# Two transformer blocks in fp32 on one core: the first half's lower-bound products of HGRN on VectorE, the low parts behind the level updates, and the last level's copy ahead of the values' copy

## The reference, cut to what matters

```python
def hgrn2_mixer(h, w_in, lb, norm_w, w_out):
    proj = h @ w_in
    q = jax.nn.silu(proj[..., :fd]).astype(jnp.float32)
    f = proj[..., fd:2 * fd].astype(jnp.float32)
    i = proj[..., 2 * fd:2 * fd + D_MODEL].astype(jnp.float32)
    g = proj[..., 2 * fd + D_MODEL:]
    f_t = lb + (1.0 - lb) * jax.nn.sigmoid(f)
    log_f = jnp.log(jnp.maximum(f_t, F_FLOOR))
    k = (1.0 - lb) * jax.nn.sigmoid(-f)
    o = hgrn2_chunkwise(q, k, log_f, i)          # decayed linear attention, by head
    o = merge_heads(head_rmsnorm(o, norm_w)).astype(h.dtype) * jax.nn.silu(g)
    return o @ w_out
```

## Time and profile before

| | |
|---|---|
| median of 3 executions | 1446.04 us (1446.02 to 1446.37) |
| the profiled execution | 1446.88 us |
| its span, first to last instruction | 1445.0 us |
| busy: PE, DVE, ACT, POOL | 1402.5 (97%), 1134.4 (79%), 784.3 (54%), 4.4 us |
| mean granted TensorE clock | 0.994 |
| loaded by DMA | 345.84 MB, 239 GB/s over the span |

### The profile page before, as it was taken

The page is one execution under the profiler, slowest core; times in us unless marked ns, Lnnn a source line. Parts: engine busy times, 40 slices in busy tenths (PEclk is TensorE's granted clock), DMA queues, the critical chain, the costliest instruction groups (busy, mean ns, idle before and its releaser), DMA issues.

```text
span 1445.0 us, 20755 instructions
## 1 busy us (share of the span) xinstructions
PE 1402.5 (97%) x8152; PEld 1184.1 (82%) x8152; DVE 1134.4 (79%) x1282; ACT 784.3 (54%) x855; POOL 4.4 (0%) x8
## 2 busy tenths in 40 slices
PE   5999999999989999999999999999999999999999
PEld 4877799899887877888888788787887787888887
DVE  3788798887877778988988988988886677666564
ACT  1535443334473656777777678675665443454442
POOL 0000000000000000000000000000000000000000
PEclk9999999999999999999999999999999999999999
DMA  9768679998463465999999999965554335355653
GB/s 356 252 251 278 228 262 337 313 304 298 142 220 117 169 213 160 366 334 310 355 345 306 344 351 339 335 248 171 179 175 146 117 117 175 117 175 192 202 167 109
DMA packets 200465, 345.84 MB, mean 239 GB/s; under 512 B 10593, under 2 KB 89025, under 8 KB 196289
## 3 DMA queue, kind: packets, MB, share of 16 engines
q1 hardware_dynamic: 193392, 338.71, 68.5%
q10 hardware_dynamic: 6992, 6.02, 1.4%
HBM read 343.66 MB, written 1.05 MB: 239 GB/s over the span
## 4 chain that ended last, share of the span: by engine, by line
PE 77%; DVE 11%; issue 4%; ACT 3%; DMA 3%; SPq 1%; DVEq 0%; ACTq 0%
PE ps L1440 20%; PE ps L1442 19%; PE ps L1441 19%; PE ps L1508 5%; DVE wlo L2384 4%; PE ps L1510 3%; ACT whi L681 2%; DMA raw<-in_m_w_in 2%; PE ps L1545 1%; PE ps L1996 1%; DMA Z<-in_ada_w 1%; PE ps L2240 1%; DVE Z L2844 1%; PE ps L2280 1%; PE ps L1486 1%
## 5 line engine op out<-in xcount | busy, mean ns | idle before, releaser
L2384 DVE TENSOR_TENSOR wlo<-raw,whi 128x2048 fp32r<-128x2048 f32 (+2 forms) x201 | 438.8, 2194 | 96.5 <-ACT whi L681 89.6
L681 ACT ACTIVATE whi<-raw 128x2048 fp32r<-128x2048 f32 (+2 forms) x201 | 369.1, 1838 | 255.3 <-PE ps L1442 198.7
L1440 PE MATMUL ps<-whi,AHL 128*128 128x512 f32 (+1 forms) x816 | 322.2, 395 | 7.3 <-DVE wlo L2384 3.8
L1441 PE MATMUL ps<-wlo,AHL 128*128 128x512 f32 (+1 forms) x816 | 312.9, 384 | 0.0
L1442 PE MATMUL ps<-whi,AHL 128*128 128x512 f32 (+1 forms) x816 | 312.8, 383 | 0.0
L1440 PEld LDWEIGHTS ps<-whi,AHL 128*128 128x128 f32 x816 | 154.2, 189 | 46.4 <-DVE wlo L2384 11.1
L1442 PEld LDWEIGHTS ps<-whi,AHL 128*128 128x128 f32 x816 | 154.1, 189 | 28.3
L1441 PEld LDWEIGHTS ps<-wlo,AHL 128*128 128x128 f32 x816 | 154.4, 189 | 24.9
L1440 PE MATMUL ps<-whi,HH 128*128 128x512 f32 x432 | 171.6, 397 | 1.1 <-DVE HL L3419 0.6
L1442 PE MATMUL ps<-whi,HL 128*128 128x512 f32 x432 | 168.4, 390 | 0.0
L1441 PE MATMUL ps<-wlo,HH 128*128 128x512 f32 x432 | 168.4, 390 | 0.0
(11 more groups left out here) (400 smaller groups left out, 1910.0 us busy)
## 6 DMA issues: line engine op xcount, KB each, us to landing
raw<-in_ada_w SPq DMA_DIRECT2D x31, 1024.0 KB, 6.2
raw<-in_w_in SPq DMA_DIRECT2D x26, 1024.0 KB, 5.1
raw<-in_moe_w_up SPq DMA_DIRECT2D x24, 1024.0 KB, 7.3
raw<-in_h_w_in SPq DMA_DIRECT2D x16, 1024.0 KB, 5.5
raw<-in_moe_w_gate SPq DMA_DIRECT2D x16, 1024.0 KB, 7.3
raw<-in_moe_w_down SPq DMA_DIRECT2D x16, 1024.0 KB, 6.0
acc<-in_moe_w_down SPq DMA_DIRECT2D x16, 1024.0 KB, 7.7
Z<-in_ada_w SPq DMA_DIRECT2D x14, 1024.0 KB, 7.1
```

Of the source, the lines that this page charges most:

```text
L681: act.activation(whi[:, h, 0:n], w.at[s][:, 0:n], ACT.Copy).then_inc(w_hi, 1)
L1440: pe.matmul(o, sh, mh, start=first, stop=False)
L1441: pe.matmul(o, sh, ml, start=False, stop=False)
L2384: dve.tensor_tensor(wlo[:, h, 0:n], w.at[s][:, 0:n], whi[:, h, 0:n].bitcast(fp), ALU.subtract)\
```

## The change

It has three parts.

1. `forget_out(0)` on ScalarE ends behind the two sigmoids. The eight scalings of the first half are done on VectorE, by the new `forget_scale`, between low part 4 (with its accumulation) and low part 5: `tensor_scalar` in place, four with multiply and add of two columns (then `f_set`), four with a multiply by one column (then the new semaphore `forget_scaled`). Step (0,0) on TensorE waits for `forget_scaled` besides `u_free`. The second half stays on ScalarE.
2. On VectorE the low parts 6 to 10 stand further behind in the order of updates and masks, and `decays(1)` between update (0,7) and low part 9 instead of ahead of update (0,6). Update (1,1) comes ahead of low part 10.
3. On ScalarE `level_out(0, 8)` comes ahead of `value_out(0)`.

```diff
--- before.py
+++ after.py
@@ -321,6 +321,7 @@
         v_set = sem("v_set")
         col_tp, cols_set = sem("col_tp"), sem("cols_set")
         m_sc, m_exp, m_pt, m_o, heads_done = (sem("m_sc"), sem("m_exp"), sem("m_pt"), sem("m_o"), sem("heads_done"))
+        forget_scaled = sem("forget_scaled")
         h_act, h_vec, f_set, u_free = sem("h_act"), sem("h_vec"), sem("f_set"), sem("u_free")
         l_kq, l_mm, l_free = sem("l_kq"), sem("l_mm"), [sem("l_free0"), sem("l_free1")]
         n_ts, n_high, h_ready = sem("n_ts"), sem("n_high"), sem("h_ready")
@@ -1149,6 +1150,8 @@
                     act.wait_ge(l_mm, H_STEPS.index((0, "r")) + 1)
                 act.activation(flatA[:, cut].rearrange("p (b n) -> p b n", b=2), src, ACT.Sigmoid)
                 act.activation(hk[:, cut].rearrange("p (b n) -> p b n", b=2), src, ACT.Sigmoid, scale=-1.0).then_inc(u_free, 1)
+                if c == 0:
+                    return
                 act.wait_ge(u_free, 2 * c + 1)
                 act.wait_ge(h_vec, 2)
                 for k in range(4 * c, 4 * c + 4):
@@ -1238,8 +1241,8 @@
             h_hi(10)
             level_out(0, 7)
             h_hi(11)
+            level_out(0, 8)
             value_out(0)
-            level_out(0, 8)
             h_hi(12)
             h_hi(13)
             level_out(1, 5)
@@ -1979,6 +1982,8 @@
                 pe.wait_ge(l_free[n % 2], n // 2)
                 if s == 0:
                     pe.wait_ge(u_free, 2 + 2 * c)
+                    if c == 0:
+                        pe.wait_ge(forget_scaled, 1)
                 else:
                     pe.wait_ge(l_kq, H_UPDATES.index((c, s)) + 1)
 
@@ -2987,6 +2992,18 @@
             both(dve.tensor_scalar(lbc[:, 8:16], lbc[:, 0:8], -1.0, 1.0, ALU.mult, ALU.add), h_vec, 2)
 
 
+            def forget_scale():
+
+                dve.wait_ge(u_free, 1)
+                for k in range(4):
+                    one = slice(SEQ * k, SEQ * k + SEQ)
+                    ins = dve.tensor_scalar(flatA[:, one], flatA[:, one], lbc[:, 8 + k:9 + k], lbc[:, k:k + 1], ALU.mult, ALU.add)
+                both(ins, f_set, 1)
+                for k in range(4):
+                    one = slice(SEQ * k, SEQ * k + SEQ)
+                    ins = dve.tensor_scalar(hk[:, one], hk[:, one], lbc[:, 8 + k:9 + k], None, ALU.mult)
+                ins.then_inc(forget_scaled, 1)
+
             def decays(c):
 
                 dve.wait_ge(f_set, c + 1)
@@ -3107,30 +3124,31 @@
             gates_out(0)
             h_lo(3)
             h_lo(4)
+            forget_scale()
             h_lo(5)
             columns_out(0)
             decays(0)
             dve.wait_ge(at_clear, 1)
-            h_lo(6)
             level_update(0, 1)
             level_mask(0, 0)
             level_update(0, 2)
+            h_lo(6)
             level_mask(0, 1)
-            h_lo(7)
             level_update(0, 3)
             level_mask(0, 2)
             level_update(0, 4)
+            h_lo(7)
             level_mask(0, 3)
-            h_lo(8)
             level_update(0, 5)
             level_mask(0, 4)
+            level_update(0, 6)
+            h_lo(8)
+            level_update(0, 7)
             decays(1)
-            level_update(0, 6)
             h_lo(9)
-            level_update(0, 7)
             level_update(0, 8)
+            level_update(1, 1)
             h_lo(10)
-            level_update(1, 1)
             level_mask(1, 0)
             level_update(1, 2)
             level_mask(1, 1)
```

## The result

The kernel after took 1438.47 us in the median of four executions (1435.11 to 1438.84), the kernel before 1446.03 (1445.71 to 1446.37): ratio 0.9946, 95% interval 0.9934 to 0.9959. That is 7.6 us less. The profiled execution took 1438.52 us, its span 1436.7.

The account below looks back on a forecast made before the run. TensorE, busy 97% of the span, was taken as the bound, with four HGRN-stage waits totalling 6.36 us. Gains 1.66 + 2.20 + 1.03 + 1.70 minus a new 1.3 us stall gave 5.3 us: 1440.7 us, range 1439.1 to 1443.4.

Parts of the forecast that it names:

- The first stall goes: TensorE's wait at (0,0) for ScalarE's query copy vanishes, 1.66 us; the eight products take 2.5 us on VectorE.
- the load of unit 5 would be there at 405.0: Load issued at 399.49 lands after the median 5.5 us, so ScalarE's high part and query copy can move up.
- the bound of 411.4: With unit 5's load 1.5 us late, ScalarE's query copy would still end by 411.4, before TensorE reaches (0,0) at 411.98.
- The second and third stall go: TensorE's waits for updates at (0,1), 2.13 us, and (0,6), 0.97 us, vanish with low parts behind the updates.
- A new stall of 1.3 us at (1,1): TensorE waits at (1,1) for the bank freed by VectorE's mask (1,0), behind update and low part 10: 1.3 us lost.
- The fourth stall goes: TensorE's 1.60 us wait at (1,2) vanishes because ScalarE copies the bank of (0,8) ahead of the values.
- The DRAIN rule: VectorE's next operation waits for an empty pipe: eight products about 3.05 us, gain some 0.5 us smaller; four 512-wide products contradict.
- The sum of 5.3 us: Total gain inside the span, taken off the median: 1.66 + 2.20 + 1.03 + 1.70 - 1.3 us.
- The clock rival: The new gap near 450 us drops TensorE to 1.2 GHz; 20 us of that gives 1450.7 us; chance 0.04.
- the updates weren't late: Rival: VectorE, with 0.4 us spare at units 6 to 8, delivers late, costing 2.8 us: 1443.5 us; chance 0.14.
- The gain lasts through the expert stage: Rival said the opposite: the expert stage's weight stream sets the end, the gain is lost, 1446.0 us; chance 0.06.
- More than forecast: Rival: mask (1,0) is done earlier than placed, gain up to 6.6 us, 1439.4 us; chance 0.04.

Follow-up runs that it names:

- Part 1 alone: Kernel before with only the eight first-half products moved to VectorE, orders as before: 1443.38 us, ratio 0.9991.
- part 2 alone: Kernel before with only VectorE's low parts put behind the updates, products still on ScalarE: 1443.36 us, ratio 0.9992.
- both other orders: Kernel after with low part 10 ahead of update (1,1), or with it behind mask (1,0): 1437.97 us each, ratios 0.9957 and 0.9952.
- both low parts behind: Kernel after with low part 10 behind mask (1,0) and low part 11 behind mask (1,2): 1437.79, 1438.61 and 1437.87 us in three comparisons.

## Why the prediction was wrong, point by point

- **The first stall goes**: right, and the products cost 2.47 us. Wrong was that the load of unit 5 would be there at 405.0. It came at 404.90 of a span that runs 2.19 us ahead, so 2.1 us later than I put it, for I used the median over all loads of this tensor, 5.5 us, as if it were this load's time. This load took 7.6 us, and 6.8 already in the trace of before, where I could have read it. It cost nothing: the query copy still had 0.6 us to spare, within the bound of 411.4 that I gave (409.16 here is 411.35 there).
- **The second and third stall go**: right, with (0,1) 4.14 us after (0,0). Part 1 alone leaves 1.60 us of the second, part 2 alone leaves all of the first.
- **A new stall of 1.3 us at (1,1)**: 1.18, and the order of update, low part and mask makes it, since both other orders take it away.
- **The fourth stall goes**: right.
- **The DRAIN rule** (The Trainium skill, VectorE: DVE Perf Modes, section on the DRAIN) would have had the eight take 3.05 us; they took 2.47, so four of a kind do overlap here too. The same section also says that an operation that isn't held (made to wait until all earlier ones have finished) starts earlier. The rows agree with that clause, not with the bare rule.
- **The step that failed** is "The sum below is a difference inside the span, so I take it off the median". The sum of 5.3 us is right: 5.43 by the stage, 5.7 +- 0.4 by the executions at equal clock. But I took the median of three executions within 0.35 us as the kernel's level and gave the range no term for the stages outside. There the clock comes and goes: before took 1442.6 to 1449.0 us on one chip. The comparison set executions of after with a mean clock of 0.996 to 0.999 against a kernel before whose profile had 0.994; the clocks of its other executions aren't known, so that this made the other 2 us is worked out from the later runs, not shown for these.
- **The clock rival** was priced on one side only, as a loss from the new gap. No profile shows a fall there. Two of the four profiles with a stall of 1.7 to 1.9 us at (0,0) show one behind *that* stall, which the change removes. Over the later runs the mean clock is 0.9952 for before and 0.9960 for after, which by the slope is 0.7 us, most of the difference between 6.5 and 5.7. That the removed stall is its cause is argued, not shown. The Trainium skill, TensorE: Matmul & The Clock Gate, Part 1, says that idling lowers the clock. The rows at 411 us and near 550 us agree with its direction; the fall at 114.0 us above came with no idle time, and at 411 us equal gaps went either way.
- **The other rivals** didn't come. No gap stands at units 6 to 8, so the updates weren't late. The gain lasts through the expert stage: the rest is 950.76 us after and 951.44 before. "More than forecast" needed the mask earlier, and it was not; moved ahead by hand (both low parts behind), it gives a stage 6.7 us shorter, where that rival said 6.6.

What stays open: whether the version with both low parts behind is faster than the kernel after. Its stage is 1.2 us shorter in three profiles of three, its executions 0.5 +- 0.4 us faster at equal clock. Against before it gave 0.9959, 0.9946 and 0.9946.

## What to carry to other kernels

Cost an edit by landmarks: the stretch between two instructions that stand on either side of it agreed within 0.4 us in all profiles of one kernel, where the whole time spread over 6 us. Put the first one behind whatever varies in front of the edit: from (0,0) on, two profiles agreed within 0.04 us. Before an edit worth less than 0.5%, take a dozen executions of the kernel before with their mean clocks; a tight group of three isn't its spread. Where an in-order engine has a product's update, a weight split and a bank's release to do, the release that TensorE waits for goes ahead of the split.

## What the runs showed of the hardware that I had not expected

Kernels with the same instructions, one semaphore declared or not, had their spells at the lower clock in other places of the span, in all between 6.8 and 20.6 us of it. A gap doesn't decide it alone: near 550 us a gap of 2.48 us left the clock at 1.00 in one profile and one of 2.07 us had it fall in another. At 114 us it fell once with no gap at all. Where TensorE would have waited anyway, a spell cost nothing ((0,1) 6.34 us after (0,0) with the one at 411 us, 6.35 without); in front of dense matmuls the one near 550 us cost 1 to 2 us.
